# Conditioning sums moved to VectorE, and the decaying heads' values computed token-major, a feature tile at a time

## The chip, the cores and the metric

One NeuronCore of a Trainium2 chip runs the whole program. The metric is device time in microseconds, the median of the runs. Engines: TensorE (PE), VectorE (DVE), ScalarE (ACT), GpSimd (POOL), and SyncE (SP), which here only starts transfers; ACT's queue starts the transfers of the first weights too.

## What is computed

Two transformer-like blocks on x, 512 tokens of 2048 features, float32. The change touches the front of the first:

```
c_act = silu(c)
mod = c_act @ w_ada + b_ada                     # 2048 x 6144
shift, scale, gate = split(mod, 3)
h = rms(x, norm_g) * (1 + scale) + shift
proj = h @ w_in                                 # 8 groups of 1024 columns: a_q a_k a_v a_z g_q g_f g_i g_z
att = chunk_attention(a_q, a_k, a_v) * silu(a_z)
hg = hgrn2(g_q, g_f, g_i) * silu(g_z)           # 8 decaying heads of 128; g_i is their values V
x = x + gate * (concat(att, hg) @ w_out)
```

A second block (three kinds of attention, one of them over 256 memory tokens `mem` by way of `mem_norm(mem) @ w_mem`) follows and isn't changed, except that its product with `w_mem` (the memory keys and values) stands at the very front of the program as work for PE while the conditioning is loaded.

## The kernel before, in words

Layout: features on the 128 partitions, tokens along the free dimension. x is 16 tiles `M.y[k]` of 128x512, h is 16 pairs of such tiles (a high part rounded to fp32r, a low part that is the remainder). Each float32 product is three fp32r matmuls: high by high, low by high, high by low. Weights come as *items*, 128x1024 each (512 KB), in a ring of three: a transfer into `wraw`, ACT rounds it to `whi` (`split`, L1143), DVE (the first 24 items, `rest_of`, L1595) or POOL makes the remainder `wlo`, PE does 24 matmuls of 512 columns (a `w_mem` item has 12). A tile of `w_in`, 128 output features, is two items: `LOW` (h tiles 0 to 7) and `HIGH` (8 to 15).

All engines run through one order, `in_order` (L464), which calls for each engine what it does there. `part` is one item. After every four feature tiles a *slot* comes, in which the small work of three lines goes on a step each: "core" (the attention or decaying head, `hg`, 11 steps), "post" (what is done to a tile that PE has finished), "slow" (the rest: the gate sums and others).

The order at the start (`START`, then `BEGUN`): sixteen memory items m0 to m15, and between them nine of the sixteen steps `ada(q)` of PE (L775), then eight `LOW` items of tiles of `w_in` begun in eight PSUM banks, with the seven other `ada` steps between them, then the `HIGH` halves of h are made and each begun tile is finished in its turn. `ada(q)` multiplies four row groups of a quarter of `w_ada`'s scale and shift columns by c: 16 fp32 matmuls of 32 columns of c (`c32`) by 512, in 32-row groups of one bank. `sums(chunk)` (L795) then turns and adds the four row groups by 32 small matmuls. The 64 transfers `w_ada` (512 KB each) sit on SP's queue in eight places and wait for `S.adq`. DVE scales x (`normed`, L1616), ACT adds the shift and rounds (`h_put`, L1245), DVE makes h's low part (L1653). So the first h tile waits for half of scale and shift, the second eight for the other half.

The gate (the last third of `w_ada`) is done on the "slow" line, `gates(g)`, in 2 x 16 steps on DVE, each a multiply-and-add of 128x1024 into `gate_acc` (L1752), six slots apart, and at the end 32 small matmuls on PE (L860).

Then for each decaying head four tiles of `w_in`: decay, hq, hv, hz. `hv` comes out feature-major, ACT evicts it, PE turns it by four transposes (`turn`, L894), DVE copies it back (L1849). `hg(h)` starts behind `hv`, and behind `hz` for head 0. Attention heads follow, four tiles each.

## Time and profile before

| | |
|---|---|
| median of 3 runs | 2632.55 us (2632.54 to 2633.64) |
| span of the profiled execution | 2632.8 us |
| PE busy | 2608.4 us (99%) |
| DVE, ACT, POOL busy | 975.2, 1094.0, 1160.9 us |
| moved | 322.9 MB, mean 123 GB/s |

The span runs from the first to the last instruction. PE's busy time counts matmuls whose ends are modelled and overlap: a 128x512 matmul is shown 0.39 us long, but the next one starts 0.23 us after it; the starts are what to read. The clock granted to PE is given as a share of full speed, 1.00 being 2.4 GHz and 0.50 being 1.2 GHz.

### The profile page before, as it was taken

How to read it: one execution, taken by the hardware profiler on the slowest of the kernel's cores; microseconds unless marked ns; L12 is line 12 of the kernel's file. 1: busy time of each engine (PE TensorE's matmuls, PEld its weight loads, DVE VectorE, ACT ScalarE, POOL GpSimd, SP SyncE). 2: the span in 40 equal slices, each digit the busy share in tenths (PEclk: the TensorE clock that was granted, in tenths of full speed). 3: DMA queues.
4: the chain of work that ended last, by engine and by line, in shares of the span. 5: the costliest groups of instructions: out<-in, count | busy, mean ns of one | idle time of the engine just before them, and what ended most of it. 6: DMA issues, size and time to landing. Idle time of an engine off the chain costs nothing.

```text
span 2632.8 us, 34583 instructions
## 1 busy us (share of the span) xinstructions
PE 2608.4 (99%) x14142; PEld 2103.2 (80%) x14142; DVE 975.2 (37%) x1569; ACT 1094.0 (42%) x1781; POOL 1160.9 (44%) x590
## 2 busy tenths in 40 slices
PE   6999999999999999999999999999999999999999
PEld 4677778878888888878888888888888888888887
DVE  3435544343333231244677343334333233311300
ACT  5344444434444442244544444445444444433311
POOL 0034343434444454453345444445555556554543
PEclk9999999999999999999999999999999999999999
DMA  9942333333333234422222332333333333333443
GB/s 386 366 156 97 105 105 104 101 109 109 115 122 98 85 108 152 144 92 80 89 80 81 104 100 97 108 102 97 110 115 112 118 107 110 117 117 114 140 147 105
DMA packets 102397, 322.92 MB, mean 123 GB/s; under 512 B 11488, under 2 KB 13536, under 8 KB 101728
## 3 DMA queue, kind: packets, MB, share of 16 engines
q1 hardware_dynamic: 98208, 306.93, 35.7%
q10 hardware_dynamic: 4032, 13.79, 1.3%
q8 instruction: 112, 1.84, 0.3%
q14 instruction: 45, 0.37, 0.0%
HBM read 303.90 MB, written 16.78 MB: 122 GB/s over the span
## 4 chain that ended last, share of the span: by engine, by line
PE 98%; DMA 1%; ACT 0%; DVE 0%; SPq 0%; issue 0%; POOL 0%; DVEq 0%; ACTq 0%
PE bank L834 29%; PE bank L836 28%; PE bank L835 28%; PE bank L1042 1%; PE bank L1031 1%; DMA TA<-in_w_ada 1%; PE bank L732 1%; PE bank L962 1%; PE bank L1025 1%; PE bank L996 1%; PE bank L765 0%; PE bank L1078 0%; PE bank L1093 0%; PE bank L902 0%; PE bank L767 0%; PE bank L766 0%
## 5 line engine op out<-in xcount | busy, mean ns | idle before, releaser
L2164 POOL TENSOR_TENSOR wlo<-wraw,whi 128x1024 fp32r<-128x1024 f32 (+3 forms) x430 | 991.1, 2306 | 1341.8 <-ACT whi L1148 1341.4
L834 PE MATMUL bank<-Hhi,whi 128*128 128x512 f32 x2848 | 1145.2, 402 | 0.6 <-DVE par L1640 0.4
L836 PE MATMUL bank<-Hhi,wlo 128*128 128x512 f32 x2848 | 1111.6, 390 | 0.0
L835 PE MATMUL bank<-Hlo,whi 128*128 128x512 f32 x2848 | 1110.7, 390 | 0.0
L1148 ACT ACTIVATE whi<-wraw 128x1024 fp32r<-128x1024 f32 (+3 forms) x454 | 457.8, 1009 | 672.0 <-PE bank L836 648.9
L834 PEld LDWEIGHTS bank<-Hhi,whi 128*128 128x128 f32 x2848 | 535.0, 188 | 124.5 <-issue 16.2
L836 PEld LDWEIGHTS bank<-Hhi,wlo 128*128 128x128 f32 x2848 | 534.6, 188 | 114.3
L835 PEld LDWEIGHTS bank<-Hlo,whi 128*128 128x128 f32 x2848 | 535.4, 188 | 107.9 <-issue 2.2
L834 PE MATMUL bank<-Ohi,whi 128*128 128x512 f32 x320 | 127.9, 400 | 0.0
L836 PE MATMUL bank<-Ohi,wlo 128*128 128x512 f32 x320 | 124.8, 390 | 0.0
L835 PE MATMUL bank<-Olo,whi 128*128 128x512 f32 x320 | 124.6, 389 | 0.0
L1718 DVE TENSOR_TENSOR TA<-bank,rows 128x512 f32<-128x512 f32 x48 | 33.1, 690 | 202.0 <-PE bank L836 202.0
L1275 ACT ACTIVATE TA<-bank 128x512 f32<-128x512 f32 x64 | 38.0, 594 | 144.2 <-PE bank L836 144.2
L1831 DVE TENSOR_TENSOR TR<-TA,TR 128x512 fp32r<-128x512 f32 x38 | 60.0, 1578 | 100.3 <-ACT TR L1356 100.2
L1370 ACT ACTIVATE TA<-bank,par 128x512 f32<-128x512 f32 x39 | 26.9, 690 | 113.9 <-PE bank L888 113.8
L1778 DVE SCALAR_TENSOR_TENSOR TA<-TA,par 128x512 f32<-128x512 f32 x48 | 46.6, 971 | 71.8 <-ACT TA L1306 69.3
L834 PEld LDWEIGHTS bank<-Ohi,whi 128*128 128x128 f32 x320 | 60.1, 188 | 13.2 <-issue 1.4
L835 PEld LDWEIGHTS bank<-Olo,whi 128*128 128x128 f32 x320 | 60.2, 188 | 13.1 <-issue 1.2
L836 PEld LDWEIGHTS bank<-Ohi,wlo 128*128 128x128 f32 x320 | 60.0, 188 | 12.7
L1750 DVE TENSOR_TENSOR TA<-bank,TA 128x512 f32<-128x512 f32 (+1 forms) x17 | 11.1, 660 | 151.6 <-PE bank L836 151.6
L1718 DVE TENSOR_TENSOR Y<-bank,rows 128x512 f32<-128x512 f32 x45 | 30.9, 687 | 92.7 <-PE bank L836 86.1
L1306 ACT ACTIVATE TA<-TA 128x512 f32<-128x512 f32 x96 | 60.9, 634 | 3.1
(270 smaller groups left out, 2548.5 us busy)
## 6 DMA issues: line engine op xcount, KB each, us to landing
wraw<-in_w_in SPq DMA_DIRECT2D x304, 512.0 KB, 3.6
TA<-in_w_ada SPq DMA_DIRECT2D x64, 512.0 KB, 8.4
wraw<-in_w_out SPq DMA_DIRECT2D x32, 512.0 KB, 3.5
wraw<-in_w_o SPq DMA_DIRECT2D x32, 512.0 KB, 3.5
wraw<-in_w_mem ACTq DMA_DIRECT2D x16, 512.0 KB, 7.5
Y<-in_w_ada SPq DMA_DIRECT2D x16, 512.0 KB, 4.5
first<-in_w_ada SPq DMA_DIRECT2D x16, 512.0 KB, 4.5
tmp_mgs<-TA SPq DMA_DIRECT2D x32, 256.0 KB, 2.1
```

The source lines that it names most:

```text
L732: m = e.matmul(out[32 * g:32 * g + 32, :], w, x, start=start, stop=stop, skip_group_check=True)
L834: e.matmul(out, hi[:, c], xhi[k], start=first and j == 0, stop=False)
L835: e.matmul(out, hi[:, c], xlo[k], start=False, stop=False)
L836: m = e.matmul(out, lo[:, c], xhi[k], start=False, stop=last and end)
L1148: e.activation(M.whi[b][:, 0:w], M.wraw[b][:, 0:w], ACT.Copy).then_inc(S.hi)
L1275: e.activation(M.dst(kind, *at), src, ACT.Copy).then_inc(S.eva)
L1306: e.activation(M.t1, M.t1, ACT.Ln, bias=1.0).then_inc(S.sg)
L1370: e.activation(W["R"], M.bST, ACT.Ln, scale=1.0 / k, bias=M.eps).then_inc(S.ln)
L1718: e.tensor_tensor(dst, src, M.rows, ALU.mult).then_inc(S.evd)
L1778: e.scalar_tensor_tensor(out=M.t2, in0=x, scalar=bias, in1=M.t1, op0=ALU.min, op1=ALU.subtract).then_inc(S.t2)
L1831: e.tensor_tensor(M.sql, M.W2["SQ"], M.sqh.bitcast(F32), ALU.subtract).then_inc(S.sql)
L2164: e.tensor_tensor(M.wlo[b][:, 0:w], M.wraw[b][:, 0:w], M.whi[b][:, 0:w].bitcast(F32), ALU.subtract).then_inc(S.lo)
```

## The change

Conditioning. `w_ada` is laid out by output feature: 48 blocks, each 128 output features (partitions) by 2048 inputs. c is made a row on every partition (`cb`, 128x2048): DVE builds `diag` (the identity times c), PE multiplies it by ones in four matmuls ahead of m1, ACT evicts. Then one DVE instruction, `tensor_tensor_reduce` of 128x2048, gives a whole 128-column piece of scale or shift, with bias and gain folded in. The blocks come through six places of 1 MB, scale and shift of one feature tile after each other. PE's `ada` and `sums` are gone. The gate is done in the same way, two halves of 1024 a block, and its closing matmuls on PE are gone.

Begun work. Behind m15 one step for each feature tile k: DVE sums, scales x[k], sums, makes a weight remainder and h[k]'s low part; PE then multiplies the four token blocks of h[k] (stationary) by a 128x1024 item of `w_in`'s value columns (moving, `w_beg`), 24 matmuls into all eight banks. After 16 steps the values of all eight heads stand token-major in the banks, ACT evicts them to `M.hv`. So a head has three tiles left (decay, hq, hz), and the turns and their copies are gone. DVE makes the first 34 remainders instead of 24, ACT's queue loads the first 37 items instead of 26. The eviction of the memory banks goes from DVE to ACT.

```diff
-CHUNKS = (2, 0, 3, 1)
-PLACES = 8
-
-START = [(x[0], int(x[1:])) for x in ("m0 m1 m2 a0 m3 m4 a1 m5 m6 a2 m7 a3 m8 m9 a4 m10 s0 m11 a5 m12 a6 m13 a7 "
-                                      "m14 s1 m15 a8").split()]
-
-
-BEGUN = ((48, 3, ()), (41, 2, (9,)), (56, 4, (10,)), (33, 5, (11,)), (49, 1, (12,)), (57, 0, (13,)), (40, 7, (14,)),
-         (32, 6, ()))
+PLACES = 6
+
+START = [(x[0], int(x[1:])) for x in ("m0 m1 m2 m3 m4 m5 m6 m7 m8 m9 m10 m11 m12 a0 m13 a1 m14 m15").split()]
+
+AHEAD = 2
+
+
+BEGUN = (1, 0, 7, 3, 4, 6, 2, 5)
+OPENED = (2, 3, 5, 6, 0, 1, 4, 7)
+
+LOADS = [(x[0], int(x[1:])) for x in ("x0 x1 x2 x3 " + " ".join(f"a{i}" for i in range(12)) + " k0 " +
+                                      " ".join(f"a{i}" for i in range(12, 32))).split()]
+
+SCRATCH = 1024
 
...
-FIRST_LOADS, FIRST_RESTS = 26, 24
-
-
-
...
+    def slots(self, k):
+        self.slot()
+        self.slot()
+        self.done("h", [k])
...
     for what, i in START:
-        do[{"m": "mem", "a": "ada", "s": "sums"}[what]](i)
-        if (what, i) == ("s", 1):
-            do["shift"](0)
-    beat.add("core", do["mem_kv"]())
-
-
-    def last_unit():
-
-        do["ada"](15)
-        yield
-        do["sums"](3)
-
-    do["h_put"](LOW)
-    for tile, bank, fours in BEGUN:
-        for i in fours:
-            do["ada"](i)
-            if i == 12:
-                do["sums"](2)
-                do["scale"](1)
-        if bank == BVV:
-            beat.add("core", last_unit())
-        if bank == BO:
-            do["shift"](1)
-            do["h_put"](HIGH)
-        do["part"]("h", LOW, bank, True, False)
-    begun = {tile: bank for tile, bank, _ in BEGUN}
+        do[{"m": "mem", "a": "ada"}[what]](i)
+    for k in range(KT):
+        do["h"](k)
+        if k == 0:
+            do["mem_kv"]()
+        do["begun"](k)
+    for t in range(8):
+        do["hv"](t)
     beat.add("slow", do["gates"](0))
+    beat.add("slow", do["mem_norm"]())
     beat.add("slow", do["mem_turn"]())
     beat.add("slow", do["gates"](1))
     for h in range(8):
-        for j, kind in ((5, "decay"), (4, "hq"), (6, "hv"), (7, "hz")):
-            if 8 * j + h in begun:
-                bank = begun[8 * j + h]
-                do["part"]("h", range(8, 16), bank, False, True)
-                close(kind, bank, h)
-            else:
-                full("h", kind, h)
-            if kind == ("hv" if h else "hz"):
-                beat.add("core", do["hg"](h))
+        for kind in ("decay", "hq", "hz"):
+            full("h", kind, h)
+        beat.add("core", do["hg"](h))
 
 
...
+        if k == 1:
+            pe.wait_ge(S.diag, 1)
+            for n, bank in enumerate((BST, BS0, BO, BVV)):
+                e.matmul(M.banks[bank], ones, M.diag[:, n * T:(n + 1) * T], start=True, stop=True).then_inc(S.cbm)
...
+    def begun(k):
+        i = beat.item
+        hi, lo = M.whi[i % NRING], M.wlo[i % NRING]
+        xhi, xlo = M.pair["h"]
+        pe.wait_ge(S.lo, i + 1)
+        pe.wait_ge(*ready[home("h", k)])
+        for n, t in enumerate(range(8) if k else OPENED):
+            bank, w, c = BEGUN[t], slice(t // 4 * T, (t // 4 + 1) * T), slice(t % 4 * P, (t % 4 + 1) * P)
+            if k == 0:
+                pe.wait_ge(*free[bank])
+            e.matmul(M.banks[bank], xhi[k][:, c], hi[:, w], start=k == 0, stop=False)
+            e.matmul(M.banks[bank], xlo[k][:, c], hi[:, w], start=False, stop=False)
+            m = e.matmul(M.banks[bank], xhi[k][:, c], lo[:, w], start=False, stop=k == KT - 1)
+            if n == 7:
+                m.then_inc(S.item)
+            elif k == KT - 1:
+                m.then_inc(S.beg)
+        beat.slots(k)
+
+    def hv(t):
+        free[BEGUN[t]] = (S.hv, t + 1)
 
...
+        if k == 1:
+            for n, bank in enumerate((BST, BS0, BO, BVV)):
+                act.wait_ge(S.cbm, n + 1)
+                e.activation(M.cb[:, n * T:(n + 1) * T], M.banks[bank], ACT.Copy).then_inc(S.cb)
...
+        act.wait_ge(S.rr, 2)
+        act.wait_ge(S.item, KT)
+        for i, bank in enumerate(MEM_BANKS):
+            tt, src = i % 2, M.banks[bank]
+            out = M.kt[tt]
+            if i >= 2:
+                out = M.kv[:, :, :, 1, tt * P:(tt + 1) * P]
+                src = src.rearrange("p (a b d) -> p a b d", a=2, b=2)
+            e.activation(out, src, ACT.Copy, scale=M.rr[:, tt:tt + 1]).then_inc(S.mkv)
+
...
+    def h(k):
+        act.wait_ge(S.xn, k + 1)
+        act.wait_ge(S.adv, 2 * k + 2)
+        act.wait_ge(S.item, beat.used[home("h", k)])
+        e.activation(M.pair["h"][0][k], M.y[k], ACT.Identity, bias=M.par[:, k:k + 1]).then_inc(S.phi)
+
+    def begun(k):
+        split(beat.item + 2)
+        load(beat.item + 4)
+        beat.slots(k)
+
+    def hv(t):
+        act.wait_ge(*((S.beg, t + 1) if t < 7 else (S.item, 2 * KT)))
+        e.activation(M.hv[:, t // 4, t % 4], M.banks[BEGUN[t]].rearrange("p (j d) -> p j d", j=4),
+                     ACT.Copy).then_inc(S.hv)
 
...
-        e.tensor_copy(M.c32.rearrange("p (a x) -> p a x", a=KT),
-                      par[:, 64:80].unsqueeze(2).to_broadcast([P, KT, 32])).then_inc(S.c32)
-        for out, a in ((M.sel, slice(0, 4)), (M.sel_half[0], slice(0, 2)), (M.sel_half[1], slice(2, 4))):
-            e.tensor_reduce(out, M.c("ident").rearrange("p (a x) -> p a x", a=4)[:, a, 0], AX, ALU.add).then_inc(S.c32)
+        e.tensor_tensor(M.diag.rearrange("p (a x) -> p a x", a=KT),
+                        M.c("ident").unsqueeze(1).to_broadcast([P, KT, P]),
+                        par[:, 64:80].unsqueeze(2).to_broadcast([P, KT, P]), ALU.mult).then_inc(S.diag)
+        e.tensor_reduce(M.sel, M.c("ident").rearrange("p (a x) -> p a x", a=4)[:, :, 0], AX, ALU.add).then_inc(S.c32)
+        e.scalar_tensor_tensor(out=par[:, 16:32], in0=M.c("b_ada", 16, 16), scalar=1.0, in1=M.c("norm_g"),
+                               op0=ALU.add, op1=ALU.mult).then_inc(S.gb)
...
+    def ada(i):
+        k, place = i // 2, i % PLACES
+        w = M.ada_slot[place]
+        dve.wait_ge(S.cb, 4)
+        dve.wait_ge(S.ada[place], 16 * (i // PLACES + 1))
+        if i % 2:
+            gain, begin, total = 1.0, M.c("b_ada", k, 1), M.par[:, k:k + 1]
+        else:
+            dve.wait_ge(S.gb, 1)
+            gain, begin, total = M.c("norm_g", k, 1), M.par[:, 16 + k:17 + k], M.par[:, 16 + k:17 + k]
+        e.tensor_tensor_reduce(out=w, in0=w, in1=M.cb, scale=gain, scalar=begin, op0=ALU.mult, op1=ALU.add,
+                               accum_out=total).then_inc(S.adv)
+
+    def scaled(k):
+        dve.wait_ge(S.xr, 2)
+        dve.wait_ge(S.adv, 2 * k + 1)
+        e.scalar_tensor_tensor(out=M.y[k], in0=M.y[k], scalar=M.par[:, 16 + k:17 + k], in1=M.xr, op0=ALU.mult,
+                               op1=ALU.mult).then_inc(S.xn)
+
+    def h(k):
+        if 2 * k >= AHEAD:
+            ada(2 * k)
+        scaled(k)
+        if 2 * k >= AHEAD:
+            ada(2 * k + 1)
+        if k:
+            rest_of(KT + k + 1)
+        dve.wait_ge(S.phi, n.up("phi"))
+        e.scalar_tensor_tensor(out=M.pair["h"][1][k], in0=M.y[k], scalar=M.par[:, k:k + 1],
+                               in1=M.pair["h"][0][k].bitcast(F32), op0=ALU.add, op1=ALU.subtract).then_inc(S.plv)
+        n.up("plv")
...
+    def begun(k):
+        if k == KT - 1:
+            rest_of(2 * KT + 1)
+        beat.slots(k)
+
...
-            i, c = j % len(places), M.par[:, 64 + j:65 + j]
-            dve.wait_ge(landed[i], 16 * (j // len(places) + 1))
-            if j == 0:
-                if g:
-                    dve.wait_ge(S.adc, 5)
-                e.tensor_scalar(M.gate_acc, places[i], c, None, ALU.mult).then_inc(S.adm)
-            else:
+            k, w = 32 + 8 * g + j // 2, places[j % len(places)]
+            begin, total = M.c("b_ada", k, 1), M.par[:, k:k + 1]
+            dve.wait_ge(landed[j % len(places)], 16 * (j // len(places) + 1))
+            if j % 2:
                 dve.wait_ge(S.adm, KT * g + j)
-                e.scalar_tensor_tensor(out=M.gate_acc, in0=places[i], scalar=c, in1=M.gate_acc, op0=ALU.mult,
-                                       op1=ALU.add).then_inc(S.adm)
-        yield from rest(3)
-        dve.wait_ge(S.adc, 5 + g)
-        cc = 4 + g
-        e.tensor_tensor(M.par[:, 8 * cc:8 * cc + 8], M.bV[:, 0:8], M.c("b_ada", 8 * cc, 8), ALU.add).then_inc(S.adp)
-        n.up("adp")
-        yield
+                begin = total
+            e.tensor_tensor_reduce(out=w, in0=w, in1=M.cb[:, j % 2 * 1024:j % 2 * 1024 + 1024], scale=1.0, scalar=begin,
+                                   op0=ALU.mult, op1=ALU.add, accum_out=total).then_inc(S.adm)
 
...
-        for a in range(4 * 16):
-            if a in (4, 6, 8, 10):
-                i = a // 2 - 2
+        for what, i in LOADS:
+            if what == "x":
                 e.dma_start(M.Y[:, i * 2048:(i + 1) * 2048], io["xT"][:, i * 2048:(i + 1) * 2048]).then_inc(S.x[i], 16)
-            if a == 44:
-                sp.wait_ge(S.plv, KT)
+            elif what == "k":
                 e.dma_start(M.masks_in.bitcast(I32), io["masks"]).then_inc(S.mask, 16)
-            sp.wait_ge(S.adq, a // 4 - 1)
-            e.dma_start(M.ada_slot[a % PLACES], io["w_ada"][CHUNKS[a // 16], a % 16]).then_inc(S.ada[a % PLACES], 16)
+            else:
+                if i == 3:
+                    sp.wait_ge(S.cbm, 4)
+                if i in (4, 5):
+                    sp.wait_ge(S.plv, 8 * (i - 3))
+                    sp.wait_ge(S.msq, 8 * (i - 3))
+                sp.wait_ge(S.adv, i + 1 - PLACES)
+                e.dma_start(M.ada_slot[i % PLACES], io["w_ada"][16 * (1 - i % 2) + i // 2]).then_inc(S.ada[i % PLACES], 16)
 
...
+            w = io["w_ada"][32 + 8 * g + j // 2][:, j % 2 * 1024:j % 2 * 1024 + 1024]
+            e.dma_start(places[j % len(places)], w).then_inc(S.adg[g][j % len(places)], 16)
```

## Rows read from the trace of the kernel before

**Rows 1.** The page: PE's busy time, and the ended-last chain by engine.

```profile
PE 2608.4 (99%) x14142; PEld 2103.2 (80%) x14142; DVE 975.2 (37%) x1569; ACT 1094.0 (42%) x1781; POOL 1160.9 (44%) x590
...
PE 98%; DMA 1%; ACT 0%; DVE 0%; SPq 0%; issue 0%; POOL 0%; DVEq 0%; ACTq 0%
```

**Rows 2.** Waits of PE, 0 to 140 us, then 140 us on (total, times, longest).

```profile
PE bank L765 <- DVE wlo L1600: 10.2, 1, 10.2
PE bank L732 <- DMA TA<-in_w_ada: 8.4, 3, 6.2
PE bank L732 <- ACT first L1194: 2.1, 1, 2.1
...
PE bank L834 <- DVE par L1640: 0.4, 1, 0.4
```

**Rows 3.** Windows: busy PE, PEld, DVE, ACT, POOL; granted clock; DMA share; GB/s.

```profile
20.00:40.00 20.00, 18.53 (x100) 10.93 (x100) 8.53 (x14) 11.90 (x25) 0.00 (x0) 0.91 1.02 412
40.00:60.00 20.00, 13.76 (x88) 6.57 (x80) 2.45 (x2) 6.28 (x12) 0.00 (x0) 0.83 0.99 392
60.00:80.00 20.00, 20.00 (x175) 12.49 (x172) 6.13 (x5) 10.41 (x17) 0.00 (x0) 1.00 0.96 354
...
140.00:160.00 20.00, 19.62 (x162) 13.18 (x161) 5.56 (x9) 8.66 (x12) 3.38 (x2) 1.00 0.38 137
```

**Rows 4.** Timeline of PE: start, length, what; the memory items.

```profile
10.23 0.77 PE L765 MATMUL bank<-whi,Hhi 128*128 128x512 f32 x1 [10.23 <-DVE wlo L1600]
...
92.79 0.71 PE L791 MATMUL bank<-par,first 128*32 128x1 f32 x64
...
96.42 1.92 PE L732 MATMUL bank<-TA 128*32 128x512 f32 x16
```

**Rows 5.** Timeline of PE: the first begun item and `ada` behind it.

```profile
98.27 0.50 PE L834 MATMUL bank<-Hhi,whi 128*128 128x512 f32 x1
...
103.98 1.92 PE L732 MATMUL bank<-TA 128*32 128x512 f32 x16
105.83 0.50 PE L834 MATMUL bank<-Hhi,whi 128*128 128x512 f32 x1
```

**Rows 6.** Timeline of PE: one fp32 matmul of 512 (two records), bulk behind.

```profile
83.27 1.12 PE L758 MATMUL bank<-first,one 128*128 128x512 f32 x2
...
84.46 0.39 PE L766 MATMUL bank<-whi,Hlo 128*128 128x512 f32 x1
```

**Rows 7.** Timeline of DVE: the setup's copy, a weight remainder, eight h remainders.

```profile
8.22 0.43 DVE L1578 COPY TA<-par 128x512 f32<-128x512 f32 x1
8.56 0.28 DVE L1581 TENSOR_REDUCE par<-cst 128x1 f32<-128x4 f32 x3
8.76 1.21 DVE L1600 TENSOR_TENSOR wlo<-wraw,whi 128x1024 fp32r<-128x1024 f32 x1
...
94.12 1.22 DVE L1600 TENSOR_TENSOR wlo<-wraw,whi 128x1024 fp32r<-128x1024 f32 x1 [0.39 <-ACT whi L1148]
95.27 5.38 DVE L1656 SCALAR_TENSOR_TENSOR Hlo<-Y,par,Hhi 128x512 fp32r<-128x512 f32 x8
```

**Rows 8.** Transfers by issuing line: KB each, median us to landing, 0 to 140 us.

```profile
Y<-in_xT SPq DMA_DIRECT2D x4, 1024.0 KB, 22.1
```

**Rows 9.** Timeline of PE: a turn of V, and the gate's column sums.

```profile
472.49 0.66 PE L902 MATMUL bank<-cst,TA 128*128 128x128 f32 x4
472.90 0.47 PE L834 MATMUL bank<-Hhi,whi 128*128 128x512 f32 x1
...
492.77 0.72 PE L791 MATMUL bank<-one,first 128*32 128x1 f32 x62
```

**Rows 10.** Groups of DVE: the gate's multiply-and-add (busy, mean ns).

```profile
L1764 DVE SCALAR_TENSOR_TENSOR first<-Y,par,first 128x1024 f32<-128x1024 f32 x15 | 19.1, 1275 | 0.0
```

**Rows 11.** Windows, columns as in rows 3, decaying heads.

```profile
220.00:260.00 40.00, 40.00 (x381) 30.89 (x381) 26.11 (x43) 19.93 (x34) 15.81 (x8) 1.00 0.32 107
```

**Rows 12.** Waits of DVE, 160 to 500 us.

```profile
DVE TA L1945 <- PE bank L962: 62.3, 39, 2.9
```

205 lines of the change are left out of this document (56 added, 149 removed).

## The prediction

> **What bounds the kernel now.** I read the page first: TensorE (PE) is busy 2608.4 of 2632.8 us and the chain that ended last is 98% PE [rows 1]. So a change pays in two coins only: PE work that goes away, and time in which PE stands still or runs at the low clock. The waits of PE say where it stands still: 10.2 us until the first weight remainder, 8.4 us for w_ada transfers, 2.1 us for ScalarE (ACT), all in the first 140 us, and after that nothing over 0.4 [rows 2]. The windows of the first 160 us show the same place from the side of the transfers: 354 to 412 GB/s at a DMA share of 0.96 to 1.02, and 137 GB/s from 140 us on [rows 3]. So the kernel has a start that is fed by DMA, and behind it some 2500 us in which every matmul more or less is time more or less. I therefore add up in three pieces: the time at which the memory items m0 to m15 end (Tm), the time at which the begun work ends (Tb), and the PE work left behind Tb. The profiled execution is 2632.8 us, the median of the runs 2632.55; I take them as equal.
>
> **Piece one, Tm.** Before, PE works from 10.23 to 96.42 us on the memory items and what is put between them [rows 4]: 86.2 us. That contains eight conditioning steps `ada` (a0 to a7) at 105.83 - 103.98 = 1.85 us each [rows 5], 14.8; the 8.4 and 2.1 us of waits [rows 2]; two `sums` at 0.65 us (the row at 92.79, 0.71 long, its successor starts at 93.43), 1.3 [rows 4]; and about 2.5 us of low clock: the granted clock is 0.91 in 20 to 40 us and 0.83 in 40 to 60 us, against 1.00 in the others, so some 3.4 and 6.8 us lay at the lower level (1.2 GHz), most of the second stretch in the longest wait for w_ada, 6.2 us [rows 2, 3]. What stays is 57.1 us. The change adds four 128x128x512 fp32 matmuls of the broadcast of c in front of m1. One such (two records) took from 83.27 to about 84.23, the next bulk matmul but one starting at 84.46 [rows 6]: 4 x 0.93 = 3.7 us. VectorE (DVE) gets a product of 2048 elements (`diag`) ahead of the first remainder, where a 512-element copy stood from 8.22 on and the remainder started at 8.76 [rows 7]. A product of 1024 takes 1.15 us from start to start (94.12 to 95.27) and one of 512 0.67 us (eight in 5.38 us), so an element costs between 0.94 ns (the difference by 512) and 1.12 ns (1.15 by 1024), and one of 2048 takes 1.15 + 1024 such, 2.1 to 2.3 us; I take 2.2. It takes the place of 0.34 us for the copy (8.22 to 8.56), and a small product joins: PE starts 1.9 us later, at 12.1. The wait of 2.1 us for ACT is mostly covered by the new matmuls; I leave 0.5. The eight a-steps and their 8.4 us of waits are gone, so is the second cold spell. Tm = 12.1 + 57.1 + 3.7 + 0.5 = 73.4 us. Bounds: 71 (nothing left of the cold start) to 78 (half-clock matmuls for the broadcast, or the weight loads slowed by the four 1 MB loads of x, which took 22.1 us to land [rows 8]).
>
> **Piece two, Tb.** From m15 on the order is one step per feature tile: DVE sums a row block of scale, scales x, sums one of shift, makes a weight remainder, makes h's low part; PE then does 24 matmuls. Three rates compete.
> PE: the 24 matmuls of an item take 103.98 - 98.27 = 5.7 us with its lead to the next operation, 5.5 in a row [rows 5].
> DMA: two blocks of 1.05 MB and one weight of 0.52 MB, 2.62 MB a step; at the 354 to 412 GB/s of the loaded windows [rows 3] 6.4 to 7.4 us. Six places are three steps of lead, enough.
> DVE: eight scalar_tensor_tensor of 128x512 took 5.38 us, 0.67 each [rows 7]; there are two a step, 1.34. The remainder of 1024 is 1.15. The two multiply-and-sums (tensor_tensor_reduce) of 128x2048 are not in the trace. From below they cost what a plain product of 2048 would, 2.1 us as above; I see no reason for less. From above, the nearest row that does two operations an element and runs beside GpSimd, 1.27 us for 1024 [rows 10], gives 2.55; a form at half the rate would be 4.3, and that is a rival. I take 2.35, between the two, since the sum has to be written out as well, and 0.15 for one wait of DVE on its own result (adv before `scaled`). A step is then 2 x 2.35 + 1.34 + 1.15 + 0.15 = 7.3 us. ACT's h lies beside DVE's remainder, its weight split beside the sums.
> So DVE sets the pace, PE waits 1.7 us in each step. The remainder of weight 17 comes 2.2 us after m14, and scaled, h and h's remainder follow, so PE starts the first step 1.6 us after Tm. Tb = 73.4 + 1.6 + 15 x 7.3 + 5.6 = 190.1 us. Bounds: 6.9 us a step (sums at 2.1, no more for the wait) gives 184, 7.9 a step (sums at 2.55 and a little lateness of DMA) 199.
>
> **Piece three, the rest.** Before, 2632.8 - 96.4 = 2536.4 us lie behind m15. Out of it go: eight more a-steps at 1.85, 14.8; two `sums` 1.3; the values tiles of the eight heads, 16 items at 5.46 us, 87.4 (they are now inside Tb); the eight turns of V, 472.90 - 472.49 = 0.41 us each, 3.3; the two column sums of the gates, 0.7 each, 1.4 [rows 9]; and some 1 us of small waits [rows 2]. 2427 us stay. Hidden at no cost: the eight evictions of V on ACT (PE's last step finishes bank after bank, and the next tiles take the first two banks), the eviction of the memory banks moved from DVE to ACT, the gate products (32 on DVE before, 32 of equal size after; 1.27 us a piece [rows 10]), the new waits on `adm` (the gates' 200 slots end before the attention's 224). SP's queue holds nothing behind its waits for `adv` but the same loads. Sum: 190.1 + 2427 = **2617 us**, 16 us or 0.6% less than before. Put another way: 37 us of PE work go, 6 come (the broadcast, and 0.14 us more an item), 2.5 us of low clock go, and the standing still grows from 22 to about 40 us.
>
> **Where a page of the skill speaks against it.** The rows first: a tensor_tensor of 1024 fp32 elements takes 1.15 us and a scalar_tensor_tensor of 512 0.67 us with both inputs in SBUF, about one element a cycle of 1 ns [rows 7]; neither carries a sum. The Trainium skill, Vector Engine (DVE) Microarchitecture Reference, section 7 (Points that are easy to get wrong), says that the scalar_tensor_tensor shape with two non-bf16 SBUF sources runs at half throughput because no port is left for the accumulator. By that rule the row of 0.67 us would be over 1.1 us, so the trace doesn't bear it out for the plain form; for one that accumulates no row decides.
>
> **Rivals.**
> (a) The multiply-and-sum runs at half the rate: 4.3 us each. A step is 2 x 4.3 + 2.63 = 11.2 us, Tb = 73.4 + 1.6 + 168 + 5.6 = 249, the end 2676 us, 1.6% slower. It decides from 2.35 + (2632.8 - 2617)/30 = 2.9 us an instruction on. For it: no row shows a summing form. Against: all rows of DVE with GpSimd idle. 10%. (It is what the sentence of the Trainium skill quoted above would make of the instruction.)
> (b) PE's clock. The begun steps leave PE still for 1.7 of 7.3 us, and the stretch behind the 2.1 us wait for ACT has a granted clock of 0.91 [rows 2, 3]. At 1.2 GHz the 24 matmuls take near 10.9 us, more than DVE's step, but then PE doesn't stand still; if half of the time lies low, a step is 5.5/0.75 = 7.3, just DVE's pace; if all, 11 us, but PE is then never idle, so it won't last. I put 5 to 10 us on it: 2622 to 2627. 15%.
> (c) The gain is lost behind the start. A head of the decaying part has 12 slots of PE work now instead of 16, 33 us for 44, while DVE's work a head stays what it was (up to 26.1 us busy in 40 [rows 11]) but for one copy. The chain is PE step, DVE products, next PE step; DVE waited 62.3 us in 39 times for PE in it [rows 12], 1.6 us of slack a step. A gate product of 1.3 us now falls on the same two slots of every head, one of them behind decay's chain. If PE waits over 1.3 us a head, eight heads take 10 us: 2627 to 2633, no change. 12%.
> (d) The multiply-and-sum as fast as its lower bound, no cold spell, and the first part shorter: 2604 to 2610. 10%, inside the range.
> That the change doesn't do what it says would show as PE's a-steps still there; the diff removes them, so I give it nothing.
>
> **Numbers.** Forecast 2617 with its own range 2608 to 2626. The range for 8 in 10 takes in (b) and most of (c), 2605 to 2637, and leaves (a) out. A measurement of this kernel can tell some 0.2%, 5.3 us, from no change: 2627.3 to 2637.8. Faster 0.74 (forecast 0.53, (b) 0.11, (d) 0.10), same 0.14 ((c), the slow end of (b)), slower 0.12 ((a) and some of (c)).
>
> **What would show it.** Tm near 73 us; the first multiply-and-sum rows at 2.3 to 2.4 us; sixteen steps 7.3 us apart, with PE's waits in them named after DVE's h remainder (about 25 us); ACT and DVE of the decaying heads busier by a third, with PE's waits there near 0. It is wrong if the rows are over 2.9 us, if PE's waits in the steps name a DMA, if the granted clock stays well under 1.00 from 75 to 190 us, or if PE waits in the stretch of the decaying heads.

## The result, and the profile after

The changed kernel takes 2655.65 us (median of 4 runs, 2653.53 to 2660.33) against 2633.1 for the kernel before on the same chip: 1.0089 times the time before, 95% interval 1.0076 to 1.0101. It is 0.9% slower; 2617 us were forecast and 2605 to 2637 was the range. The profiled execution has a span of 2654.3 us.

The page, its busy times and its chain that ended last, beside [rows 1]:

```profile
PE 2584.6 (97%) x13478; PEld 2096.5 (79%) x13478; DVE 1081.6 (41%) x1654; ACT 1095.7 (41%) x1785; POOL 1134.4 (43%) x580
...
PE 90%; DVE 7%; ACT 1%; issue 1%; DMA 1%; POOL 0%; SPq 0%; DVEq 0%; ACTq 0%
```

PE has 24 us less work than before (2608.4 to 2584.6), and the kernel is longer by 22. So PE stands still more, and the waits of PE say where. First 0 to 220 us, then from 220 us on (total, times, longest), beside [rows 2]:

```profile
PE bank L777 <- DVE Hlo L1627: 22.5, 15, 1.7
PE bank L754 <- DVE wlo L1583: 12.7, 1, 12.7
PE bank L714 <- ACT first L1164: 4.3, 2, 3.1
PE bank L777 <- issue: 2.0, 1, 2.0
...
PE bank L937 <- DVE TA L1909: 19.6, 7, 2.8
PE bank L928 <- DVE TA L1909: 5.8, 7, 0.8
```

The first four lines are the forecast's start: PE waits 1.5 us in each of 15 begun steps. The next two are not in its sum: in the decaying heads PE waits 25.4 us, seven times 2.8 and seven times 0.8, for line 1909, a product of `hg` on DVE. Before, nothing in that stretch was over 0.4 us [rows 2].

The start, in the timeline of PE: the broadcast of c, the last memory matmul and the first begun one, the first matmul behind the begun work.

```profile
17.48 3.60 PE L726 MATMUL bank<-TA,one 128*128 128x512 f32 x8
...
76.54 0.39 PE L756 MATMUL bank<-wlo,Hhi 128*128 128x512 f32 x1
78.93 0.47 PE L777 MATMUL bank<-whi,Hhi 128*128 128x512 f32 x1 [2.00 <-issue]
...
192.52 0.39 PE L813 MATMUL bank<-Hhi,whi 128*128 128x512 f32 x1
```

The memory items end at 76.77 us and the begun work at 192.5. One begun step in the timeline of DVE, from sum to sum:

```profile
93.12 2.41 DVE L1609 CUSTOM_DVE_ANT_0 TA<-TA,cb,par 128x2048 f32<-128x2048 f32 x1
95.45 0.09 DVE L1609 DVE_READ_ACCUMULATOR2_ANT par<- 128x1 f32 x1
95.57 0.75 DVE L1615 SCALAR_TENSOR_TENSOR Y<-Y,par,rows 128x512 f32<-128x512 f32 x1
96.24 2.34 DVE L1609 CUSTOM_DVE_ANT_0 TA<-TA,cb,cst 128x2048 f32<-128x2048 f32 x1
...
98.51 1.22 DVE L1583 TENSOR_TENSOR wlo<-wraw,whi 128x1024 fp32r<-128x1024 f32 x1
99.65 0.74 DVE L1627 SCALAR_TENSOR_TENSOR Hlo<-Y,par,Hhi 128x512 fp32r<-128x512 f32 x1
100.31 2.40 DVE L1609 CUSTOM_DVE_ANT_0 TA<-TA,cb,par 128x2048 f32<-128x2048 f32 x1
```

From 93.12 to 100.31 are 7.19 us, with DVE idle nowhere for as much as 0.1 us: 7.3 were forecast.

Behind the begun work 2654.3 - 192.5 = 2461.8 us pass, where 2427 were forecast: 34.8 us too many. Windows of it (columns as in rows 3), two of 20 us and three of 120 us, all in the decaying heads:

```profile
240.00:260.00 20.00, 17.20 (x163) 13.05 (x162) 12.22 (x22) 8.85 (x19) 6.83 (x3) 1.00 0.29 104
...
300.00:320.00 20.00, 17.20 (x80) 13.98 (x79) 5.58 (x9) 7.52 (x13) 6.00 (x3) 0.91 0.16 53
...
260.00:380.00 120.00, 111.91 (x1028) 87.22 (x1026) 60.40 (x100) 50.40 (x83) 43.78 (x21) 0.97 0.25 89
380.00:500.00 120.00, 109.97 (x977) 85.54 (x971) 63.15 (x111) 51.65 (x89) 41.06 (x19) 0.96 0.26 89
500.00:620.00 120.00, 115.55 (x945) 91.28 (x944) 60.57 (x106) 54.55 (x96) 43.51 (x20) 0.99 0.25 88
```

PE is busy for 17.2 us in either window of 20 us, for each holds a wait of 2.8 us. Behind six of the seven such waits the clock falls: the matmuls of 512 columns then start 0.43 us apart and not 0.23, the granted clock of such a window is 0.91 (once 0.98 and 0.94 in two neighbours), and PE loses about 1.6 us each time by its starts. Behind the first, which ends at 257.67 us, it does not: 1.00 from 240 to 260 and from 260 to 280 us. In the windows between (280 to 300, 320 to 340 and 360 to 380 us) it is 1.00. The shares missing from 1.00 in the three long windows make 120 x (0.03 + 0.04 + 0.01) = 9.6 us. Waits of 25.4 and 9.6 of clock are 35.0 us: they account for the 34.8. The clock's part is rounded to the two digits of the column; the windows of 20 us would give 10.6, and six times 1.6 us is 9.6.

What happens in such a window, around 301 us: the timelines of DVE, then of GpSimd (POOL), then of PE.

```profile
299.23 0.49 DVE L1784 TENSOR_SCALAR TA<-TA,par 128x512 f32<-128x512 f32 x1 [0.70 <-ACT TA L1316]
299.63 1.28 DVE L1733 CUSTOM_DVE_ANT_0 Y<-Y,cb,cst 128x1024 f32<-128x1024 f32 x1
...
300.83 0.43 DVE L1907 TENSOR_TENSOR TA<-TA 128x256 f32<-128x256 f32 x1
301.17 2.57 DVE L1909 TENSOR_TENSOR TA<-TA 128x256 f32<-128x256 f32 x1
...
301.10 2.35 POOL L2126 TENSOR_TENSOR wlo<-wraw,whi 128x1024 fp32r<-128x1024 f32 x1 [6.57 <-ACT whi L1114]
...
303.88 1.19 PE L937 MATMUL bank<-TA 128*128 128x128 f32 x4 [2.80 <-DVE TA L1909]
```

The decay chain (lines 1780 to 1784, paced by ACT) ends late; behind it stands a gate product (L1733, 1.28 us); then the two products on which PE's next step of the head waits. The second of them starts 0.07 us behind a weight remainder of GpSimd (301.17, 301.10), and its row is 2.57 us long where it is usually 0.42. Its median over 56 is 418 ns and its mean 958. It ends 0.3 us after the end of GpSimd's row. PE waits 2.80 us. Of that the gate product alone makes some 0.65 us (2.80 less the 2.15 by which the product is too long): an estimate, to be compared with pool256 below.

Why every time: a head now has 12 slots, the gate products come every 6, so they meet the same two slots of each head, the first and the seventh; the decay chain is in the seventh. Before, a head had 16 slots and the two periods drifted against each other. So far this is a reading of one trace. Four questions are for the chip: whether the meeting is the cause, whether both its parts (the gate product, GpSimd) are needed, whether it is bound to the changed kernel, and what limits the begun steps.

### The profile page after: what moved, and what is told of

Read it like the earlier page. It is cut to its first block, busy times and chain, and to the rows that moved or that the text cites. A ratio compares the mean times of both kernels' runs of the same rounds, so it can differ in the third digit from the quotient of the medians.

```text
span 2654.3 us, 33281 instructions
## 1 busy us (share of the span) xinstructions
PE 2584.6 (97%) x13478; PEld 2096.5 (79%) x13478; DVE 1081.6 (41%) x1654; ACT 1095.7 (41%) x1785; POOL 1134.4 (43%) x580
## 4 chain that ended last, share of the span: by engine, by line
PE 90%; DVE 7%; ACT 1%; issue 1%; DMA 1%; POOL 0%; SPq 0%; DVEq 0%; ACTq 0%
PE bank L813 27%; PE bank L815 26%; PE bank L814 26%; DVE TA L1609 2%; PE bank L1008 1%; PE bank L997 1%; DVE TA L1909 1%; DVE first L1609 1%; PE bank L928 1%; PE bank L991 1%; DVE wlo L1583 1%; PE bank L962 1%; DMA wraw<-in_w_mem 1%; DVE Y L1733 1%; DVE Y L1615 0%
## 5 line engine op out<-in xcount | busy, mean ns | idle before, releaser
L2126 POOL TENSOR_TENSOR wlo<-wraw,whi 128x1024 fp32r<-128x1024 f32 (+3 forms) x420 | 963.8, 2295 | 1386.0 <-ACT whi L1114 1385.8
L813 PE MATMUL bank<-Hhi,whi 128*128 128x512 f32 x2720 | 1097.5, 403 | 0.2 <-POOL Hlo L2236 0.2
L815 PE MATMUL bank<-Hhi,wlo 128*128 128x512 f32 x2720 | 1063.6, 391 | 0.0
L814 PE MATMUL bank<-Hlo,whi 128*128 128x512 f32 x2720 | 1063.4, 391 | 0.0
L813 PEld LDWEIGHTS bank<-Hhi,whi 128*128 128x128 f32 x2720 | 513.2, 189 | 114.4 <-issue 9.9
L815 PEld LDWEIGHTS bank<-Hhi,wlo 128*128 128x128 f32 x2720 | 512.1, 188 | 109.9
L814 PEld LDWEIGHTS bank<-Hlo,whi 128*128 128x128 f32 x2720 | 513.0, 189 | 103.5 <-issue 2.2
L777 PE MATMUL bank<-whi,Hhi 128*128 128x512 f32 x128 | 51.1, 399 | 24.5 <-DVE Hlo L1627 22.5
L815 PEld LDWEIGHTS bank<-Ohi,wlo 128*128 128x128 f32 x320 | 60.0, 188 | 12.7
```

What stands on the lines that cost most here:

```text
L777: e.matmul(M.banks[bank], xhi[k][:, c], hi[:, w], start=k == 0, stop=False)
L813: e.matmul(out, hi[:, c], xhi[k], start=first and j == 0, stop=False)
L814: e.matmul(out, hi[:, c], xlo[k], start=False, stop=False)
L815: m = e.matmul(out, lo[:, c], xhi[k], start=False, stop=last and end)
L2126: e.tensor_tensor(M.wlo[b][:, 0:w], M.wraw[b][:, 0:w], M.whi[b][:, 0:w].bitcast(F32), ALU.subtract).then_inc(S.lo)
```

## Experiments

The expectations set two theories against each other. Theory C: the loss is a coincidence of three jobs, decay's chain, a gate product behind it and GpSimd's remainder. Theory D: twelve slots a head are too few for DVE's work, wherever the gate product lies (in the kernels made from the one before: sixteen slots absorb the meeting). In the edits a line with - is the kernel named, one with + the experiment. Ratios are to the kernel before on the same chip, with 95% intervals.

### shift3: the gate products moved to other slots

```diff
     for t in range(8):
         do["hv"](t)
+    beat.add("slow", rest(3))
     beat.add("slow", do["gates"](0))
```

> The changed kernel with three empty slots ahead of the first gate product, nothing else: the gate products fall on slots 4 and 10 of each decaying head instead of 1 and 7. Theory C (collision): in slot 7 of every head VectorE does decay's chain, then a gate product (1.28 us), and its next product of hg is so late that it meets GpSimd's weight remainder on the way (2.57 us instead of 0.42); TensorE waits 2.8 us and then gets a spell at the lower clock. With the gate product elsewhere the 25.4 us of waits and the six low spells (3.4 us each) behind 220 us go: 2617 to 2624 us, PE waits there under 5 us. Theory D (density): twelve slots a head are too few for VectorE's work, wherever the gate product lies; then the waits move to another slot and 2645 to 2656 us stay.

Measured: 2620.25 us, 0.9952 (0.9935 to 0.9968). A line of three empty steps takes four slots, so the gate products came on slots 5 and 11, and not on 4 and 10 as the expectation has it. Behind the begun work only this wait of PE and one as long for GpSimd are left:

```profile
PE bank L929 <- DVE TA L1910: 0.2, 1, 0.2
```

and the first of the long windows shows the clock whole (the second does too):

```profile
260.00:380.00 120.00, 119.98 (x1162) 93.17 (x1161) 66.51 (x117) 55.74 (x94) 48.95 (x23) 1.00 0.30 102
```

The end of the decay chain in the same head, in the timeline of DVE:

```profile
295.20 0.49 DVE L1785 TENSOR_SCALAR TA<-TA,par 128x512 f32<-128x512 f32 x1 [0.70 <-ACT TA L1317]
...
295.93 0.42 DVE L1910 TENSOR_TENSOR TA<-TA 128x256 f32<-128x256 f32 x1
...
297.54 2.23 DVE L1927 TENSOR_TENSOR TA<-TA 128x256 f32<-128x256 f32 x1 [1.11 <-PE bank L938]
```

With no gate product in between, both products are over before GpSimd begins (297.07 us). The last row shows that a product is still held now and then, 2.23 us, but in a step with slack, and PE doesn't wait for it. The work is the same, the bytes are the same, only the place of 32 small instructions and their loads differs, and 35 us go. The first matmul behind the begun work starts at 192.21 us, so 2619.1 - 192.2 = 2426.9 us lie behind: the forecast's 2427.

### gate64: the gate products in place, but short

Of each gate product only 64 of 1024 elements are multiplied and summed, so the gate isn't the reference's.

```diff
-            e.tensor_tensor_reduce(out=w, in0=w, in1=M.cb[:, j % 2 * 1024:j % 2 * 1024 + 1024], scale=1.0, scalar=begin,
+            e.tensor_tensor_reduce(out=w[:, 0:64], in0=w[:, 0:64], in1=M.cb[:, 0:64], scale=1.0, scalar=begin,
```

> The changed kernel with gate products of 64 elements instead of 1024 (the gate's sums are left out but for these 64), on the same slots. Theory C: 1.2 us less in slot 7, so VectorE's next product starts at about 299.8 instead of 301.17 us, ahead of GpSimd's remainder: no wait, 2614 to 2622 us. A theory in which GpSimd alone holds VectorE: the blocked product stays 2.3 to 2.7 us long in each head and the waits stay near 15 us or more.

Measured: 2620.5 us, 0.9954 (0.9938 to 0.9970). The instruction, its waits and its slot are all there; its length alone is gone, and with it all the waits of PE on line 1909. Line 1909 in this run, then in the changed kernel (duration in ns: shortest, median, longest):

```profile
L1909 DVE TENSOR_TENSOR TA<-TA x56: 410/418/424, 233.7 to 552.3; 128x256 f32<-128x256 f32 x56
```

```profile
L1909 DVE TENSOR_TENSOR TA<-TA x56: 411/418/2608, 232.2 to 586.3; 128x256 f32<-128x256 f32 x56
```

So it is the 1.2 us by which the gate product pushes the product behind it into GpSimd's remainder, and GpSimd alone, whose remainders are as long as before, holds none of the 56 rows.

### pool256: the gate products in place, GpSimd's remainders short

GpSimd computes 256 of the 1024 columns of each weight remainder below item 84, so the low part of those weights is left out.

```diff
-            b, w = j % NRING, ITEMS[j][3]
+            b, w = j % NRING, 256 if j < 84 else ITEMS[j][3]
```

> The changed kernel with GpSimd's weight remainders cut to 256 of 1024 columns for the items of the decaying heads (the rest of each low part is left out). Theory C: the product of hg behind the gate product takes 0.4 to 0.9 instead of 2.57 us, TensorE's wait falls from 2.8 to 0.5 to 1.2 us a head, and without a wait over 2 us the low spells go: 2622 to 2634 us. Theory D (VectorE too full by its own work): the waits fall by little, 2645 us or more.

Measured: 2629.07 us, 0.9985 (0.9975 to 0.9996), 26.6 us less than the changed kernel. Waits of PE behind the begun work, and the meeting in the timelines of DVE and of GpSimd:

```profile
PE bank L937 <- DVE TA L1909: 8.2, 7, 1.2
...
298.96 0.94 DVE L1909 TENSOR_TENSOR TA<-TA 128x256 f32<-128x256 f32 x1
...
298.89 0.73 POOL L2126 TENSOR_TENSOR wlo<-wraw,whi 128x256 fp32r<-128x256 f32 x1 [8.20 <-ACT whi L1114]
```

DVE's product is again held until GpSimd's ends, but that is 0.5 us now and not 2.15. What is left is 1.2 us a head, and 0.5 of it is still GpSimd's; the gate product alone costs some 0.65 us a head behind the chain (1.17 - 0.52 here, 2.80 - 2.15 in the changed kernel), since 0.55 of its 1.2 us is slack. Rival (c) was priced at 1.3. The first slot's waits are gone altogether. The granted clock is 1.00 in every window of 20 us from 240 to 600 us: none of the seven waits of 1.2 us is followed by low clock here, six of the seven of 2.8 us are. The run with 2.8 us waits is 26.6 us longer, of which 17.2 are wait and some 9.6 clock.

### slots5: the gate products five slots apart

```diff
-GATE_SLOTS = 6
+GATE_SLOTS = 5
```

> The changed kernel with a gate product every 5 slots instead of every 6. By 12 slots a head the 16 products of the first gate half then fall on slots 6, 11, 4, 9, 2, 7, 12, 5, 10, 3, 8, 1, 6, 11, 4, 9, so only one (head 2) falls on slot 7, where all heads had one before. Theory C: one wait of 2.8 us for the last hg step of VectorE's products and perhaps one low spell, waits behind 220 us 3 to 6 us, 2618 to 2626 us. Theory D: the work for VectorE in the heads is denser still (products follow each other faster), waits stay at 20 us or more, 2645 to 2660 us.

Measured: 2627.47 us, 0.9984 (0.9974 to 0.9994), 28.2 less than the changed kernel and 1.5 above the range expected under theory C. With 5 against 12 the gate products drift through the slots, and the meeting happens once in full. The longest wait of PE behind the begun work:

```profile
PE bank L937 <- DVE TA L1909: 2.8, 1, 2.8
```

PE's waits in the decaying heads are 6.0 us in all. The profiled execution is the fastest of the eight (a span of 2624.0 us) and has a granted clock of 1.00 throughout, behind the wait of 2.8 us too; the slower ones show 0.997 to 0.999 over the whole run, so some of the spread is clock.

### The meeting put into the kernel before: before_hz, before_meet, before_meet5

If it is a coincidence of slots, the kernel before must lose by it as well, though it has neither the new sums nor heads of 12 slots. In the first of three kernels only the start of `hg` is moved, behind `hz` in all heads, as the change has it:

```diff
-            if kind == ("hv" if h else "hz"):
+            if kind == "hz":
```

> The kernel before with hg(h) behind hz for every head, gate products every 6 slots as they were. By 16 slots a head one of them (head 4) falls on slot 7. Theory C: 2633 to 2638 us, one wait of 2 to 2.8 us. If moving hg behind hz is harmful by itself, waits in every head and 2645 us or more.

Measured: 2637.4 us, 1.0017 (1.0007 to 1.0027). With 6 against 16 slots one head is met: one wait of PE of 2.8 us for line 1947, the product that is 1909 in the changed kernel, and behind it a window (340 to 360 us) with a granted clock of 0.83.

The second adds gate products eight slots apart in the first half of the gate and four in the second (both periods divide 16), with empty steps ahead to bring them to the slot of the chain:

```diff
+def gate_slots(g):
+    return 4 if g else 8
...
+    beat.add("slow", rest(6))
     beat.add("slow", do["gates"](0))
...
-            yield from rest(GATE_SLOTS)
+            yield from rest(gate_slots(g))
```

> The collision built into the kernel before, which has neither the new conditioning nor the token-major values: hg(h) starts behind hz for every head, and the first gate half's products come every 8 slots from slot 15 on (the second half's every 4), so that in the heads 2 to 7 one falls on slot 7, behind decay's chain, as in the changed kernel. Theory C: six waits of TensorE of 2 to 2.8 us for VectorE's product and up to six low spells of 1.6 us: 2632.8 + 12 to 27, 2645 to 2660 us. Theory D (density: the loss comes from twelve slots a head instead of sixteen): no change, 2631 to 2636 us.

Measured: 2637.5 us, 1.0019 (1.0009 to 1.0029). It missed its aim: a line of six empty steps takes seven slots, so the gate products fell on the slot behind the chain. There GpSimd holds another product, and the steps of that slot have slack:

```profile
295.04 0.42 DVE L1953 TENSOR_TENSOR TA<-TA 128x256 f32<-128x256 f32 x1
...
295.45 1.28 DVE L1770 SCALAR_TENSOR_TENSOR first<-Y,par,first 128x1024 f32<-128x1024 f32 x1
296.64 2.64 DVE L1970 TENSOR_TENSOR TA<-TA 128x256 f32<-128x256 f32 x1
...
296.18 2.82 POOL L2170 TENSOR_TENSOR wlo<-wraw,whi 128x1024 fp32r<-128x1024 f32 x1 [6.58 <-ACT whi L1154]
...
299.76 1.10 PE L985 MATMUL bank<-TA 128*128 128x256 f32 x4 [0.44 <-DVE TA L1973]
```

The third puts it one slot earlier, and that is all the difference to the second:

```diff
-    beat.add("slow", rest(6))
+    beat.add("slow", rest(5))
```

> The kernel before with before_meet's edit, one slot earlier: the empty steps on the slow line take six slots and not seven, so that the gate products lie four slots apart on slots 3, 7, 11 and so on of the second to seventh head, slot 7 being the one of the decay chain; a head's steps start behind hz, as in the changed kernel. In before_meet they lay on slot 8, behind the chain, 2637.5 us. Theory C (the loss is a coincidence: decay chain, a gate product just ahead of its last product on VectorE, and a remainder of GpSimd that holds that product): up to six waits of PE of 1.2 to 2.8 us behind L945's or L971's kind (the decaying heads' matmuls), with low clock behind the long ones: 2645 to 2660 us, 0.4 to 1% above the kernel before. Theory D (the loss needs the changed kernel's shorter heads of twelve slots; in sixteen slots the same meeting is absorbed): 2637 us, as before_meet, with waits under 1 us.

Measured: 2656.53 us, 1.0094 (1.0077 to 1.0111), 19 us above its neighbour and as slow as the changed kernel. Timelines of DVE, GpSimd and PE, then the waits of PE and a window:

```profile
293.34 1.28 DVE L1770 SCALAR_TENSOR_TENSOR first<-Y,par,first 128x1024 f32<-128x1024 f32 x1
...
294.87 2.56 DVE L1953 TENSOR_TENSOR TA<-TA 128x256 f32<-128x256 f32 x1
...
294.81 2.34 POOL L2170 TENSOR_TENSOR wlo<-wraw,whi 128x1024 fp32r<-128x1024 f32 x1 [6.56 <-ACT whi L1154]
...
297.58 0.68 PE L977 MATMUL bank<-TA 128*128 128x128 f32 x4 [2.79 <-DVE TA L1953]
...
PE bank L977 <- DVE TA L1953: 13.9, 5, 2.8
...
400.00:420.00 20.00, 17.21 (x98) 13.54 (x97) 11.52 (x18) 9.04 (x18) 5.08 (x3) 0.91 0.24 80
```

The same rows in the same order and the same 2.8 us, with the old form of the gate product and 16 slots to a head. Five heads are met, and behind four of the five waits a window has 0.91, as the one shown; behind the first, whose rows are above, the clock stays at 1.00 (280 to 320 us), as in the changed kernel. Theory C's condition is met and its time comes; theory D, that 16 slots absorb it, falls.

### sum1024: what limits the begun steps

On shift3; the sums go over 1024 of the 2048 inputs, so scale and shift are those of half of c.

```diff
-        e.tensor_tensor_reduce(out=w, in0=w, in1=M.cb, scale=gain, scalar=begin, op0=ALU.mult, op1=ALU.add,
+        w = w[:, 0:1024]
+        e.tensor_tensor_reduce(out=w, in0=w, in1=M.cb[:, 0:1024], scale=gain, scalar=begin, op0=ALU.mult, op1=ALU.add,
```

> Built on shift3 (2620.25 us). The multiply-and-sums of scale and shift take 1024 of the 2048 elements (half of each sum is left out). If VectorE sets the pace of the sixteen begun steps, its step falls from 7.19 to 7.19 - 2 x 1.07 = 5.05 us, below TensorE's 5.5: the 21 to 22 us of TensorE's waits for h's low part go (or turn into waits for the transfers, which need 6.4 to 7.4 us a step at 354 to 412 GB/s), and the time is 2598 to 2602 us; if the transfers take over, 2604 to 2616 us with waits that name them. If VectorE doesn't set the pace, 2620 us.

Measured: 2597.97 us, 0.9867 (0.9849 to 0.9885), 22 less than shift3. PE's waits for h's low part fall from 20.9 us in 14 times to

```profile
PE bank L778 <- DVE Hlo L1629: 2.7, 5, 0.6
```

and the transfers come up to PE's pace, 418 GB/s at a DMA share of 1.01, with PE busy all the time:

```profile
100.00:120.00 20.00, 20.00 (x90) 16.57 (x89) 19.06 (x28) 6.38 (x8) 0.00 (x0) 1.00 1.01 418
```

So the sums' length was the limit of the begun steps, as forecast, and with it gone the three rates of the forecast are nearly level: from 140 to 160 us, at 419 GB/s, PE is busy for 17.9 of 20 us, and DVE waits for blocks of `w_ada` 7.3 us in all.

### ahead6, best, lead6: less of the sums in the begun steps

On shift3, six sums stand among the memory items and not two:

```diff
-START = [(x[0], int(x[1:])) for x in ("m0 m1 m2 m3 m4 m5 m6 m7 m8 m9 m10 m11 m12 a0 m13 a1 m14 m15").split()]
+START = [(x[0], int(x[1:])) for x in ("m0 m1 m2 m3 m4 m5 a0 m6 m7 a1 m8 a2 m9 m10 a3 m11 m12 a4 m13 a5 m14 m15").split()]
...
-AHEAD = 2
+AHEAD = 6
```

> Built on shift3 (2620.25 us). Six multiply-and-sums instead of two lie between the memory items, where VectorE is busy less than half. Four of 2.4 us leave the chain of the begun steps: 9.6 us less, 2610 us, TensorE's waits for h's low part 11 to 13 us instead of 21. Rival: VectorE is late with the memory items' remainders for it, and 3 us or more come back as waits for them: 2613 to 2618 us.

Measured: 2617.56 us, 0.9941 (0.9926 to 0.9956): 2.7 us of the 9.6 that four sums take, where all 9.6 were expected. The time lies in the range of the expectation's rival, but for another reason: the waits for h's low part fall to 17.8 us only. The first begun steps, freed of their sums, are not paced by DVE any more: it stands still for ACT's rounding of the weight, which waits for PE.

```profile
88.71 1.23 DVE L1584 TENSOR_TENSOR wlo<-wraw,whi 128x1024 fp32r<-128x1024 f32 x1 [3.57 <-ACT whi L1115]
```

Two steps at PE's 5.5 us and not DVE's 7.2 are worth 3.4 us, no more (an estimate from the two step times). *best* is ahead6 with the first weight remainder put ahead of `diag` on DVE (the call of `rest_of(0)` two instructions earlier in the setup):

> shift3 with ahead6, and VectorE makes the first weight remainder before the 2048-element product diag instead of after it. TensorE starts at 10.3 us instead of 12.3 to 12.7. If the memory items are bound by TensorE all of it comes through: 2608 us. If they wait for the transfer of the third and fourth weight either way, the start changes and the end doesn't: 2610 us. Against the kernel before 0.990 to 0.992.

Measured: 2614.9 us, 0.9932 (0.9920 to 0.9944). It beats both kernels, by 0.7 and 1.5%, but is 5 to 7 us above what was expected, since it starts from ahead6, which missed by 7.6. PE's first wait is 10.8 us and not 12.7. *lead6* is best with the lead of six kept through all steps, by sums for the step three further on:

> Built on best (2614.9 us): the multiply-and-sums keep a lead of six through all steps, so that VectorE, which idled in the first steps of best behind the weight ring, sums for later ones there, and the last three steps have no sums. In best 17.8 us of TensorE's waits stay, in twelve steps of 7.19 us. VectorE's work behind the memory items is 13 steps of 7.19 and three of 2.5 us; TensorE is the bound in the last three: 1.6 + 12 x 7.19 + 4 x 5.5 = 110 us where best takes 185.84 - 75 = 111 us. So 2612 to 2615 us, TensorE's waits 15 to 18 us: hardly better. If VectorE's idle time was the loss in best, 2610 us.

Measured: 2615.66 us, 0.9941 (0.9927 to 0.9954): no better, as expected. Thirteen of the sixteen steps still have two sums, and PE's waits for h's low part stay at 17.7 us.

### poolrest: the begun steps' weight remainders on GpSimd

On shift3, DVE makes 18 remainders and not 34, to shorten its step by 1.15 us.

```diff
-FIRST_LOADS, FIRST_RESTS = 37, 34
+FIRST_LOADS, FIRST_RESTS = 37, 18
...
     def begun(k):
+        remainder(beat.item + 2)
```

> Built on shift3 (2620.25 us). The sixteen weight remainders of the begun steps go from VectorE (1.15 us each) to GpSimd (2.3 to 2.4 us each), which is idle there. If the two engines only worked beside each other, a step would fall to 6.04 us and the time to 2603 us. By the rows in the decaying heads, where a VectorE product that met GpSimd's remainder took 2.57 us instead of 0.42, VectorE is held for up to 2.2 us a step: 7.19 - 1.15 + 1.3 to 2.2, that is 2623 to 2636 us, with some VectorE rows 1 to 2.2 us longer than now.

Measured: 2647.88 us, 1.0057 (1.0038 to 1.0075), 28 more than shift3 and 12 above the slow end of what was expected. DVE's rows, then GpSimd's:

```profile
123.23 2.40 DVE L1610 CUSTOM_DVE_ANT_0 TA<-TA,cb,par 128x2048 f32<-128x2048 f32 x1
...
125.67 2.76 DVE L1616 SCALAR_TENSOR_TENSOR Y<-Y,par,rows 128x512 f32<-128x512 f32 x1
...
123.55 4.33 POOL L2127 TENSOR_TENSOR wlo<-wraw,whi 128x1024 fp32r<-128x1024 f32 x1 [4.66 <-ACT whi L1115]
```

The two engines take turns: GpSimd's remainder, 2.35 us otherwise, is 4.33 long, since it is given out in the middle of a sum; the product behind the sum takes 2.76 us in place of 0.75. DVE has an instruction less in each step, and the step grows from 7.2 to 9.0 us (119.36 to 128.35 from one shift sum to the next). The expectation had counted DVE's part of this alone, and not that GpSimd is held first. This looks like the mechanism of the heads, in another place. The Trainium skill, SBUF — State Buffer (SBUF: two separate sides), says that a VectorE instruction with two SBUF inputs and a GpSimd instruction that reads SBUF contend for a shared pair of ports under an exclusive lock, held by whichever starts first for the whole instruction. The rows agree so far as DVE's product is held until GpSimd's end (0.42 becomes 2.57 beside a row of 2.35), and GpSimd's by a sum (2.35 becomes 4.33: the 1.98 more are about the 2.08 us from its start to the sum's end).

## Why the prediction was wrong, point by point

**Piece one, Tm.** 76.8 us for 73.4, inside its bounds. PE starts at 12.7 for 12.1, and the broadcast takes 3.4 us for 3.7, counted by starts as the forecast did (its row shows 3.60 by a modelled end). The term that was mis-sized is "the wait of 2.1 us for ACT is mostly covered; I leave 0.5": there are two such waits, 1.2 and 3.1 us. The longer is a transfer's in truth:

```profile
38.17 1.06 ACT L1114 ACTIVATE whi<-wraw 128x1024 fp32r<-128x1024 f32 x1 [2.61 <-DMA wraw<-in_w_mem]
```

ACT stood 2.6 us for a memory weight in a stretch of 417 GB/s, and its squares for PE came behind it; the window from 40 to 60 us has a granted clock of 0.91, 1.8 us that the sum didn't have. That the loads of x and of the conditioning pushed the weight back is a reading that no run tests; the bounds named the loads of x, the sum left both out. +0.6, +3.8 and +1.8; the other terms together were 2.8 too high.

**Piece two, Tb.** 192.5 for 190.1, of which 3.4 is Tm's; the steps themselves are 1.0 better. The sums' rows are 2.34 and 2.41 us with 0.08 us to read the accumulator behind (forecast 2.35), the step 7.19 (7.3), PE's waits 22.5 us (about 25), named after DVE's h remainder, as said. A gap of 2.0 us ahead of the first step stands for the 1.6. sum1024 shows that the reason was right and not only the number. Rival (a) falls with these rows, and the sentence of the Trainium skill behind it (half throughput with two SBUF sources) isn't borne out for this instruction: 2.35 us for 2048 elements is one element in 1.15 ns, with the sum in it. It shows in the trace under a name of its own (CUSTOM_DVE_ANT_0), and no run has a `scalar_tensor_tensor` that accumulates. Rival (b) doesn't happen here: from 80 to 180 us PE is busy 15.4 to 16.5 of 20 us, and the granted clock is 1.00 in all five windows. In shift3, with the same begun work, it is 0.97 from 60 to 80 and 0.95 from 80 to 100 us, right behind the gap of 2.0 us, and 1.00 from then on: some 1.6 us, not 5 to 10.

**Piece three, the rest.** The failed step is the list "hidden at no cost", and in it one item: the gate products, "32 on DVE before, 32 of equal size after". Their size is equal (1.28 us), their place is not: the runs show 34.8 us in its stead, 25.4 of waits for the product behind them and 9.6 of low clock. Everything else in that piece held: with the gates four slots on (shift3), 2426.9 us remain where 2427 were forecast, and the whole is 2620.25 for 2617.

**Rival (c)** named this place in so many words, the two slots of every head and the one behind decay's chain, and got three things wrong.
- The price. It put 1.3 us on a head, the length of the gate product. Alone that would cost some 0.65 us (pool256), for 0.55 is slack. But a delay of 1.2 us on DVE isn't a delay of as much on PE when it moves a product from in front of a GpSimd remainder to behind its start: GpSimd's row then comes on top, 1.2 + 2.15 - 0.55, and PE waits 2.8. The rows of before had it to be read. Line 1947's shortest, median and longest duration in ns:

```profile
L1947 DVE TENSOR_TENSOR TA<-TA x56: 410/418/1517, 187.8 to 552.1; 128x256 f32<-128x256 f32 x56
```

  One product of 0.42 us that takes 1.52 in the very same form is a sign of something held (it starts at 230.99 us, 0.25 behind a GpSimd product of 1.48), and I read means only.
- The other slot, the first of a head, costs too: 0.8 us each, 5.8 in all. It was priced at nothing. The product is held there as long (2.61 us from 278.05, GpSimd's row starts at 277.88), but PE has work until 279.98 us, 1.9 us longer than the product's start; in the seventh slot it has run out at 301.09, before the product starts.
- The clock. (b) looked for it in the begun steps, (c) had none. It was in the heads, 9.6 us.

So (c) was 7 x (2.8 + 0.8) + 9.6 = 35 us where it was priced 10 to 16.

**The chance.** (c) had 12%. DVE's load was argued from its busy share, 26 of 40 us [rows 11], which was no argument either way; the question was whether the two periods divide each other, 6 and 12, and they do. A fixed pattern makes a coincidence either never or always. That could have been counted from the slots in the diff, and would have made (c) the likeliest but for its price. The last check named ("wrong if PE waits in the stretch of the decaying heads") is the one that came true. "Busier by a third" did not: DVE is busy 66.5 of 120 us in shift3's heads and was 52 to 56 in the kernel before, a fifth to a good quarter more. A head isn't 33 us for 44 either: the chain's last row comes every 42.5 us in shift3 and every 53.5 in the kernel before, since the head's own matmuls stand between the items.

**What is shown and what isn't.** That the meeting costs the 35 us is shown by moving or shortening the gate product (35.4 and 35.2 us come back), by shortening GpSimd's part (26.6), and by adding the meeting to the kernel before. That the product is held by GpSimd's instruction rests on the order and ends of rows in three kernels and on pool256, where a shorter remainder frees it sooner. What decides whether the low clock follows a stop stays open, and its length alone doesn't: six of seven stops of 2.8 us have it in the changed kernel, four of five in before_meet5 and none of one in slots5, while the stop of 2.07 us that ends at 19.87 us in the kernel before and the gap of 2.0 us in shift3 have it too, and the gap of 2.0 us in the changed kernel doesn't.

## What to carry to other kernels

When a change alters the length of a repeating unit, write down the periods of everything that rides along with it: with periods that divide each other, a rare meeting becomes one in every round, or none, and moving one line by a few slots can be worth more than the change itself (35 us here, against 12 that the change gives with the line moved). A small instruction put on VectorE has to be priced by what GpSimd holds behind it, and not by its own length; the longest duration of a form beside its median shows where that is already happening. And work taken off VectorE and given to GpSimd can lengthen VectorE's step.
